# Merging the routing scores with the expert activation stage: one block, shared buffers, and GpSimd's subtract cut in four

## The reference, cut to what matters

```python
q = (xb @ wq).reshape(PEER_BLOCK, PEER_HEADS, 2, PEER_HALF)
s = jnp.einsum('thpd,hpkd->thpk', q, subkeys).astype(jnp.float32)
s_top, i_top = lax.top_k(s, PEER_TOPK)
cand = (s_top[:, :, 0, :, None] + s_top[:, :, 1, None, :]).reshape(...)
g_s, g_i = lax.top_k(cand, PEER_TOPK)
e = jnp.take_along_axis(cand_idx, g_i, axis=-1)
g = jax.nn.softmax(g_s, axis=-1).astype(xb.dtype)
act = jax.nn.gelu(jnp.einsum('thed,td->the', u[e], xb))
return jnp.einsum('the,thed->td', g * act, v[e])
```

## Time and profile before

| | |
|---|---|
| median of 3 runs | 2461.23 us (2456.18 to 2461.99) |
| the profiled execution | 2459.62 us, its span 2458.0 us |
| mean granted clock of TensorE | 0.909 |
| busy: PE, PEld, DVE, ACT, POOL | 86%, 69%, 68%, 35%, 38% of the span |
| scores, activation, experts | about 940 to 1108, 1108 to 1897, 1897 to 2458 us |

### The profile page before, as it was taken

How to read it: one execution, slowest core, us unless ns; L and a number is a source line. 1 busy time by engine, 2 the same in 40 slices (tenths; PEclk the granted TensorE clock), 3 DMA queues, 4 the chain that set the end, 5 groups by cost and what they waited for, 6 DMA issues and landing times. The chain is left out here.

```text
span 2458.0 us, 32103 instructions
## 1 busy us (share of the span) xinstructions
PE 2118.9 (86%) x10417; PEld 1703.5 (69%) x10417; DVE 1667.0 (68%) x2980; ACT 853.3 (35%) x1717; POOL 942.2 (38%) x727
## 2 busy tenths in 40 slices
PE   8998986687987767979799889887886999999997
PEld 7774773343435636859798889877885788888885
DVE  3562106868230133797989999988665898898888
ACT  1231012133100121113566576546553333333331
POOL 1000342222100000014677677766676566444440
PEclk9999997678899678989899999998997999999998
DMA  5323438866604102126687788778888999999993
GB/s 189 77 55 110 130 97 285 295 211 216 244 23 143 56 0 75 61 69 193 193 278 263 251 260 278 264 235 268 279 286 281 394 388 391 395 389 389 385 386 131
DMA packets 243759, 547.72 MB, mean 223 GB/s; under 512 B 22174, under 2 KB 126287, under 8 KB 242346
## 3 DMA queue, kind: packets, MB, share of 16 engines
q1 hardware_dynamic: 114538, 287.33, 33.9%
q0 software_dynamic: 60736, 208.40, 23.5%
q10 hardware_dynamic: 68352, 50.34, 6.3%
HBM read 485.51 MB, written 60.02 MB: 222 GB/s over the span
## 5 line engine op out<-in xcount | busy, mean ns | idle before, releaser
L2404 PE MATMUL psum<-hH,uH 128*128 128x384 f32 x1024 | 365.3, 357 | 76.7 <-ACT acts L2218 36.2
L2079 POOL DMA_INDIRECT u_gather<-in_u_rows,gather_ids x160 | 218.4, 1365 | 546.6 <-DVE gather_ids L1889 419.3
L2196 POOL TENSOR_TENSOR uL<-u_raw,uH 128x1024 fp32r<-128x1024 f32 x125 | 320.6, 2565 | 129.5 <-ACT uH L2210 126.3
L2404 PE MATMUL psum<-hL,uH 128*128 128x384 f32 x1024 | 355.4, 347 | 0.0
L2404 PE MATMUL psum<-hH,uL 128*128 128x384 f32 x1024 | 355.2, 347 | 0.0
L2301 DVE CUSTOM_DVE_ANT_0 u_prod<-u_gather,h 128x1024 f32<-128x1024 f32 x160 | 283.6, 1773 | 81.8 <-DMA u_gather<-in_u_rows,gather_ids 73.6
L2512 POOL DMA_INDIRECT v_gather<-in_v_rows,idx_now x160 | 237.9, 1487 | 247.1 <-DVE y_sample L2597 154.7
L2644 PE MATMUL psum<-vH,wH 128*128 128x512 f32 x768 | 301.9, 393 | 18.0 <-DVE wL L2590 18.0
L2644 PE MATMUL psum<-vH,wL 128*128 128x512 f32 x768 | 301.2, 392 | 0.0
L2644 PE MATMUL psum<-vL,wH 128*128 128x512 f32 x768 | 301.0, 392 | 0.0
L2404 PEld LDWEIGHTS psum<-hH,uH 128*128 128x128 f32 x1024 | 203.4, 199 | 82.9 <-issue 60.4
(11 more groups left out here) (485 smaller groups left out, 3463.2 us busy)
## 6 DMA issues: line engine op xcount, KB each, us to landing
u_raw<-in_uT SPq DMA_DIRECT2D x128, 512.0 KB, 4.4
S<-in_v_rows SPq DMA_DIRECT2D x64, 512.0 KB, 10.6
v_rest<-in_v_rows SPq DMA_DIRECT2D x64, 512.0 KB, 6.7
activation_table<-acts ACTq DMA_DIRECT2D x128, 192.0 KB, 4.2
gate_table<-Gtile ACTq DMA_DIRECT2D x48, 512.0 KB, 8.0
S<-gate_table SPq DMA_DIRECT2D x16, 768.0 KB, 8.0
S<-activation_table SPq DMA_DIRECT2D x16, 768.0 KB, 11.8
G_rest<-gate_table SPq DMA_DIRECT2D x16, 768.0 KB, 7.4
```

Of the source, the lines that this page charges most:

```text
L2079: c.nc.gpsimd.indirect_dma_start(c.ug[:, k % RG], None, c.A["u_rows"].rearrange("j i d -> (j i) d"), bass.IndirectOffsetOnAxis(ap=c.ids[:, ...
L2196: nc.gpsimd.tensor_tensor(uL[:, n % RU], u[:, n % RAW], uH[:, n % RU].bitcast(F32), ALU.subtract).then_inc(u_split, 1)
L2404: ins = nc.tensor.matmul(bank[n % 2][:, 0:ND], w[:, n % RU, d], x[:, d], start=m == 0, stop=m == len(parts) - 1)
```

## The change: what it does

- `stage_scores` becomes `score_programs`, which returns one function for each engine. `stage_activate` calls them at the start of its own block, so that no engine waits for the others between the scores and the activation. `hT` stays until the end of the activation.
- To make room, tensors share buffers: `wq`, `subkeys`, `qp` and `S_first` lie in `Gtile`; `hot` and `S_first_last` in `hT`; `slot_ij`, `slot_gate`, `res` and `idf` in constants that are no longer used. The product of a dot is written over the fetched row instead of to `u_prod`. Two waits are added for it: ScalarE waits for `h_split` ahead of the last head's first score copy, VectorE for the last `s_ev` ahead of the activation.
- `RG` is 5, so five fetches can be under way.
- `column`: the columns' sums use four PSUM banks (0, 1, 6, 7) in turn and not two; TensorE waits for the gelu of four columns before.
- `low_u`: GpSimd's subtract of a column, 128 x 1024, becomes four of 128 x 256. The semaphore counts behind the last.
- `STEP_COLS`: tile 0 has 12 columns and not 8, tile 3 has 28 and not 32.
- `tile_gates(0)` moves from step 5 of tile 0 to step 7.

```diff
-STEP_COLS = ((1,) * 8, (5, 5, 5, 5, 5, 5, 4, 4), (5,) * 8, (4,) * 8)
+STEP_COLS = ((2, 1) * 4, (5, 5, 5, 5, 5, 5, 4, 4), (5,) * 8, (4, 3) * 4)
...
-RG = 4
+RG = 5
...
+def low_u(c, n):
+
+    for d in range(0, KD, 2):
+        ins = c.nc.gpsimd.tensor_tensor(c.uL[:, n % RU, d:d + 2], c.u[:, n % RAW, d:d + 2],
+                                        c.uH[:, n % RU, d:d + 2].bitcast(F32), ALU.subtract)
+    ins.then_inc(c.u_split, 1)
...
-        slot_ij, slot_g, prod = sb("slot_ij", [P, PUNIT, 2, UNIT]), sb("slot_gate", [P, 2, P]), sb("u_prod", [P, D])
+        slot_ij = c.bcol[:].rearrange("p b n -> p (b n)").rearrange("p (u q t) -> p u q t", u=PUNIT, q=2)
+        slot_g = [c.tri, c.low]
...
+        pool_scores, sp_scores, pe_scores, act_scores, dve_scores = score_programs(
+            c, G[:].rearrange("p a j t -> p (a j t)"))
+        column = [bank[i] for i in (0, 1, 6, 7)]
...
-                    routed = st == (0 if p else 5)
+                    routed, gates = st == (0 if p else 5), st == (0 if p else 7)
...
-                        if routed and i == 1:
+                        if gates and i == 1:
                             tile_gates(p)
...
             @block.gpsimd
             def _(pool):
+                pool_scores(pool)
+
                 def columns(n):
                     n += AHEAD
                     if n < NKEYS:
                         pool.wait_ge(u_hi, n + 1)
-                        nc.gpsimd.tensor_tensor(uL[:, n % RU], u[:, n % RAW], uH[:, n % RU].bitcast(F32),
-                                                ALU.subtract).then_inc(u_split, 1)
+                        low_u(c, n)
...
-                    V.tensor_tensor_reduce(out=prod[:], in0=c.ug[:, k % RG], in1=c.h[:, STILE if s == GS else 0],
+                    V.tensor_tensor_reduce(out=c.ug[:, k % RG], in0=c.ug[:, k % RG], in1=c.h[:, STILE if s == GS else 0],
...
                 def columns(n):
                     pe.wait_ge(u_split, n + 1)
-                    if n >= 2:
-                        pe.wait_ge(u_act, n - 1)
+                    if n >= 4:
+                        pe.wait_ge(u_act, n - 3)
...
-            stage_scores(c)
-            hTs.close()
             stage_activate(c)
+        hTs.close()
         stage_experts(c)
```

More of the change, by code:

```diff
@@ new lines, in score_programs @@
+    sizes = (RING * KD * P, NJ * NKEYS, 2 * NT, 2 * ROUTED * NKEYS)
+    ends = list(itertools.accumulate(sizes))
+    part = [room[:, end - n:end] for n, end in zip(sizes, ends)]
+    wq = part[0].rearrange("p (i k n) -> p i k n", i=RING, k=KD)
+    sk = part[1].rearrange("p (j n) -> p j n", j=NJ)
+    qp = part[2].rearrange("p (i n) -> p i n", i=2)
+    S0 = part[3]
+    SS = c.route.SS
+    sk_in, q_mm, q_ev = c.sem("sk_in"), c.sem("rq_mm"), c.sem("rq_ev")
+    wq_in = [c.sem(f"wq_in{i}") for i in range(RING)]
@@ new lines, in pe_scores, with scores @@
+    def pe_scores(pe):
+        def scores(j):
+            pe.wait_ge(q_ev, j + 1)
+            if j == 0:
+                pe.wait_ge(sk_in, 16)
+            if j >= 2:
+                pe.wait_ge(s_ev, 2 * (j - 1))
+            quarter = slice(j // 2 % 4 * NS, (j // 2 % 4 + 1) * NS)
+            for t in range(NTILE):
+                dst = bank[4 + j % 2][:, t * P:(t + 1) * P] if t < STILE else bank[6 + j % 2][quarter, 0:P]
+                ins = nc.tensor.matmul(dst, qp[:, j % 2, cols(t)], sk[:, j], start=True, stop=True)
+            ins.then_inc(s_mm, 1)
+        for j in range(NJ):
+            pe.wait_ge(wq_in[j % RING], 16 * (j // RING + 1))
+            if j >= 2:
+                pe.wait_ge(q_ev, j - 1)
+            for q in range(2):
+                for k in range(KD):
+                    ins = nc.tensor.matmul(c.pair(j % 2)[:, q], wq[:, j % RING, k],
+                                           c.hT[:, k, q * HALF:(q + 1) * HALF],
+                                           start=k == 0, stop=k == KD - 1)
+            ins.then_inc(q_mm, 1)
+            if j:
+                scores(j - 1)
+        scores(NJ - 1)
@@ new lines, in dve_scores @@
+    def dve_scores(dve):
+        V = nc.vector
+        for k in range(KD):
+            V.tensor_copy(hH[:, k], c.hT[:, k, P:SEQ]).then_inc(h_split, 1)
+            dve.wait_ge(h_split, 2 * k + 1)
+            V.tensor_tensor(hL[:, k], c.hT[:, k, P:SEQ], hH[:, k].bitcast(F32), ALU.subtract).then_inc(h_split, 1)
+        dve.wait_ge(h_split, 2 * KD)
+        b = c.route
+        router = Router(c, dve, Link(dve, d_own))
+        for h in range(ROUTED):
+            dve.wait_ge(s_ev, 4 * (h + 1))
+            keys = slice(h * 2 * NKEYS, (h + 1) * 2 * NKEYS)
+            router.head(S0[:, keys], b.first, h, c.res0)
+            router.head(S[:, 0, keys], b.second, h, b.res)
+            if h == BATCH - 1:
+                router.convert(b.first, BATCH)
+                for i in range(BATCH):
+                    router.pick(i, c.res0)
+                router.rows_of(c.res0, 0, 64, c.ids[:, 0:NG // 2, 0:GS])
+                router.convert(b.second, BATCH)
+                for i in range(BATCH):
+                    router.pick(i, b.res)
+                router.head(SS[:, 0], b.sample, 0, c.resS)
+        dve.wait_ge(s_ev, 4 * PH)
@@ L2037 @@
+    return pool_scores, sp_scores, pe_scores, act_scores, dve_scores
 TB = 32
@@ L2217, in columns @@
                         act.wait_ge(a_stored[n % RA], 16 * (n // RA))
-                    nc.scalar.activation(a[:, n % RA], bank[n % 2][:, 0:ND], ACT.Gelu_apprx_tanh).then_inc(u_act, 1)
+                    nc.scalar.activation(a[:, n % RA], column[n % 4][:, 0:ND], ACT.Gelu_apprx_tanh).then_inc(u_act, 1)
                     act.wait_ge(u_act, n + 1)
```

186 lines of the change are left out of this document (64 added, 122 removed).

## The result

| | us |
|---|---|
| before, median of 5 runs | 2461.23 (2456.18 to 2462.75) |
| after, median of 5 runs | 2436.57 (2435.52 to 2445.76) |
| ratio, with its 95% interval | 0.992 [0.9894, 0.9941]: faster, by 0.6 to 1.1% |
| forecast | 2407 (2350 to 2447) |
| after, profiled span, mean granted clock | 2434.7, 0.919 |

A forecast was written before the change was run, and what follows sets the result against it. The prediction took VectorE, sharing an exclusive SBUF port with GpSimd, as the bound, TensorE second. From 2459.6 us it took 14.5 for the start and 38 for tiles 1 to 3, giving 2407 us, range 2350 to 2447.

The forecast's parts named there:

- The seam: Between scores and activation: TensorE runs nothing for 16 us; merging the blocks lets columns start at about 1092 us.
- D: Rival on the subtract's pieces: they do nothing, each port wait still lasts a whole subtract; 2429 us, chance 0.16.
- Start-up: Up to tile 1's transposes: merged blocks start columns earlier, transposes end at 1182.4 instead of 1196.9 us; gain 14.5 us.
- Tiles 1 to 3: Rest of the activation stage, 701 us: pieces let VectorE and GpSimd fill each other's port gaps; 663 us, gain 38.
- 15 us for the pieces' own cost: Tiles 1 to 3: the pieces' fixed cost, 0 to 61 us, mostly hidden while VectorE has the port; a quarter taken.
- 10 us of fetch waits: Tiles 1 to 3: VectorE's waits for fetched rows fall from 74 us as a fifth buffer lets fetches run ahead.
- the 2452 us: Time forecast if the pieces' fixed cost, 187 ns by a rule from the Trainium skill, were exposed in full, 60 us.
- The fifth buffer: Fetched rows, mainly tile 3: lets GpSimd run one dot further ahead; counted as 10 us in D.
- Four banks: Column sums in PSUM: remove 36 us of TensorE's waits for ScalarE's column activation, but priced at 0.
- TensorE isn't last: Tiles 1 to 3: TensorE's own 531 us lie under the 663 us forecast, so its waits don't set the time.
- Rival C: GpSimd becomes the bound, its pieces queueing behind VectorE's instructions: 727 us for tiles 1 to 3, 2471 in all, chance 0.15.
- B: Rival: the hand-over works better, common off-port time falls to 30 us and the pieces' cost vanishes; 2349 us, chance 0.14.

The follow-up runs named there:

- iota in PSUM: The changed kernel, four pieces, with VectorE's one-hot builds reading iota from a PSUM bank into which ScalarE copies it once: 2410.7 us.
- fetch ahead, one: The changed kernel with GpSimd's fetch issued ahead of its column's subtract, and the subtract in one piece: 2410.1 us.
- fetch ahead, two: The changed kernel with GpSimd's fetch issued ahead of its column's subtract, and the subtract in two pieces: 2400.2 us.
- fetch ahead, four: The changed kernel, four pieces, with only GpSimd's order turned round, the fetch ahead of the subtract: 2427.2 us.
- fetch ahead and iota, two: The changed kernel with the subtract in two pieces, the fetch ahead of it, and one-hot builds reading iota from PSUM: 2366.4 us.
- fetch ahead and iota, four: The changed kernel, four pieces, with the fetch ahead of the subtract and one-hot builds reading iota from PSUM: 2395.0 us.

## Why the prediction was partly right

**Right.** The bound: VectorE and GpSimd on one port, TensorE second. The seam: columns at 1092.4 (forecast about 1092), worth 16 us by itself. The wait ahead of the gates is gone. The time fell, as forecast, and the experts are within 3 us. D's mechanism is out as a whole: pieces hand the port over most of the time; but 14 instructions met it. Its outcome for the pieces, that they gain nothing, was near.

**Start-up, forecast 14.5 us, measured 8.8.** From the first column matmul to the transposes the forecast had 21 x 4.16 + 1.5 = 88.9 us; it took 95.1. The changed kernel's trace shows what the 6 us are, GpSimd and TensorE in order of time and then the busy times of 6 us:

```profile
1168.89 1.42 POOL L2079 DMA_INDIRECT u_gather<-in_u_rows,gather_ids  x1 [6.14 <-DVE dots L2320]
1170.33 5.87 POOL L2087 TENSOR_TENSOR uL<-u_raw,uH 128x256 fp32r<-128x256 f32 x4
...
1176.25 0.69 PE L2425 MATMUL psum<-hH,uH 128*128 128x384 f32 x1 [2.92 <-POOL uL L2087]
...
1176.00:1182.00 6.00, 5.75 (x18) 5.75 (x19) 4.97 (x19) 1.06 (x1) 5.66 (x7) 0.50 0.54 180
```

GpSimd's fetch waited 6.14 us for a dot, and the four pieces behind it took 5.87 us, as VectorE's dots got the port in between. So TensorE waited 2.92 us for uL, and behind this pause its granted clock was 0.50 for about 6 us, the 1.2 GHz level: its matmuls started every 0.32 us and not every 0.17. With two pieces the fetch waited 6.13 us too, but the two pieces took 2.53 us, TensorE was busy in all of the stretch, and it took 90.0 us. The waits that the pieces moved to GpSimd reached TensorE here. This is one profile of each kernel; others with 21 columns had 90 to 99 us.

**Tiles 1 to 3, forecast 38 us, measured 11.5: the steps that failed are "15 us for the pieces' own cost" and "10 us of fetch waits".** The forecast took the pieces to be worth 22 us (its 2407 against D's 2429). The runs give 1 us (2436.6 against 2437.7). It priced their cost at a quarter of the upper end, since "most of it hides while VectorE has the port". Two pieces run back to back in 2.49 us and four in 2.80, one in 2.34: 0.15 us for each further one. The trace shows the 2.49 in this row of the two-piece kernel, GpSimd in order of time:

```profile
1186.30 2.49 POOL L2087 TENSOR_TENSOR uL<-u_raw,uH 128x512 fp32r<-128x512 f32 x2
```

In 107 columns four pieces take GpSimd 107 x 0.46 = 49 us more than one. How much of that shows can be read from the traces: *in use* below is the time in tiles 1 to 3 in which a subtract of GpSimd or a dot or other two-operand elementwise instruction of VectorE is in progress (working or waiting for the other; one-hots with iota in PSUM left out), *neither* is the remainder. "Subtracts" is 107 times (110 in the kernel before) the shortest duration of a column's subtract, and the last column VectorE's waits for rows.

| kernel | tiles 1 to 3 | subtracts | in use | neither | waits for rows |
|---|---|---|---|---|---|
| before | 700.8 | 257 | 546.0 | 154.8 | 73.6 |
| one piece | 686.7 | 250 | 537.5 | 149.2 | 68.0 |
| two | 680.6 | 266 | 546.0 | 134.6 | 83.1 |
| four (the change) | 689.3 | 300 | 563.4 | 125.8 | 139.8 |
| fetch ahead, one | 654.1 | 250 | 536.5 | 117.6 | 33.9 |
| fetch ahead, two | 649.5 | 266 | 545.1 | 104.4 | 46.1 |
| fetch ahead, four | 682.9 | 300 | 565.8 | 117.1 | 118.4 |
| fetch ahead and iota, two | 616.3 | 266 | 467.1 | 149.2 | 49.6 |
| fetch ahead and iota, four | 648.4 | 300 | 497.8 | 150.6 | 137.3 |

Of the 49 us, 26 show as time in which the port's users are at work (537.5 to 563.4), where the sum had 15; about half hides, where the forecast had most of it. Against it the time of neither fell by 23 us (149.2 to 125.8), and the two cancel. The forecast had 251 + 300 + 15 = 566 us for the first, which the measured 563.4 meets partly by luck: with one piece it was 13.5 us less than 251 + 300 already. For the second it had 73 + 13.6 + 10 = 97 us, and that is where the distance lies: 125.8. VectorE working off the port makes 37 of it (forecast 73; 80 before), and waiting for rows 64 (forecast 10; 49 before); the rest is shorter waits, 7 us for the last exponential among them.

From two to four pieces the timed kernels lose 27 us with the fetch ahead and 29 with iota in PSUM too. In their profiles the first loss is 21 us of use and 13 us of neither, the second 31 us of use. So from one piece to two the relief is larger than the price, and from two to four it is smaller. The table has one profile for each kernel.

With the full price, 46 to 49 us where the sum had 15, the forecast would be 2438 to 2441, near the measured 2436.6; by the table that agreement is luck. The same holds for the 2452 us that the prediction gave beside it. That estimate was worked out from the 4497 ns for 2048 elements of the Trainium skill (GPSIMD Engine Reference, "3.1 Elementwise"); the 187 ns of fixed cost that follow are near the 0.15 us of these runs, but in the changed kernel they aren't exposed in full.

**"10 us of fetch waits", measured 139.8 in all.** Its picture was that a fetch is late for want of a buffer. What stands ahead of the fetch makes it late, a column's subtract that now keeps GpSimd 3.95 us and not 2.57: 68.0 us of waits with one piece, 83.1 with two and 139.8 with four. And there is a circle; in tile 3 of the changed kernel, in order of time:

```profile
1702.19 0.69 ACT L2279 ACTIVATE hT<-hT,tri 128x128 f32<-128x128 f32 x2 [8.14 <-DVE hT L2348]
...
1703.56 1.04 ACT L2227 ACTIVATE uH<-u_raw 128x1024 fp32r<-128x1024 f32 x1
...
1704.67 3.44 POOL L2087 TENSOR_TENSOR uL<-u_raw,uH 128x256 fp32r<-128x256 f32 x4 [5.52 <-ACT uH L2227]
...
1708.25 0.94 POOL L2079 DMA_INDIRECT u_gather<-in_u_rows,gather_ids  x1
...
1713.90 1.64 DVE L2320 CUSTOM_DVE_ANT_0 u_gather<-u_gather,h 128x1024 f32<-128x1024 f32 x1 [8.45 <-DMA u_gather<-in_u_rows,gather_ids]
...
1715.47 1.48 DVE L2348 TENSOR_TENSOR hT<-iota,bcol 128x768 f32<-128x768 f32 x1
...
1716.98 0.69 ACT L2279 ACTIVATE hT<-hT,tri 128x128 f32<-128x128 f32 x2 [6.09 <-DVE hT L2348]
```

ScalarE's gate multiply waits 8.14 us for a one-hot; the next uH stands behind it; GpSimd's subtract waits 5.52 us for that uH; the fetch stands behind the subtract; VectorE waits 8.45 us for the row; the next one-hot stands behind that dot; and ScalarE waits again, 6.09 us. Each engine works in order, and the circle closes. Tile 3 holds 103.2 of the 139.8 us and didn't get shorter with four columns less. The circle existed before the change (20 us from the order alone); the forecast took most of its waits as recoverable by the buffer, and the pieces lengthened them. Issuing the fetch ahead cuts the circle, but with four pieces 118 us of waits stay, so there GpSimd's load is most of the cause.

**Terms too low.** The fifth buffer: 10 us forecast (in D), 14 measured. Four banks: 0 forecast, 7 measured, not clear of the noise; undone, TensorE waits 27.5 us for ScalarE's column activation again, though 25.7 instead of 53.1 for uL. "TensorE isn't last" was too coarse: at tile 1's start it is, where VectorE waits 6.81 us for its transposes.

**Rival C** was nearer in its signs than in its time. GpSimd came to 0.90 of tiles 1 and 2, VectorE waited for rows and TensorE for uL. But GpSimd's subtracts lost 134 us to VectorE where C had 174, and of the pieces' cost 26 us showed where C had 61. **B**'s off-port time of 30 us was never reached; the lowest was 104.

**The best version** has the merge and the side parts of the change, two pieces, the fetch ahead of the subtract, and iota in PSUM: 2366.4 us, 70 us faster than the change and 94 faster than before.

## What to carry to other kernels

Cutting an instruction on a shared port buys shorter waits with a fixed cost for each piece, and it shortens one engine's waits by lengthening the other's: multiply that cost by the number of pieces, expect half of it or more to show when both engines are nearly full, look for what waits behind the engine that got slower, and try two pieces before four. Here taking one operand off the port was worth more (26 us) than slicing (1 to 10 us). Where an engine waits for data that another queue fetches, look at what stands ahead of the fetch in that queue and what that in turn waits for; if it leads back to the first engine, put the fetch ahead.

## What the runs showed of the hardware

- Back-to-back pieces of GpSimd hand the port over in most cases, not in all: at 1317.15 a VectorE comparison waited through four pieces, and at 1157.07 one took 6.24 us for 0.7, longer than the eight pieces beside it (5.6 us). 12 of the 14 long waits began within 0.08 us of the start of a piece. Whether that decides it wasn't tried.
- A subtract of 128 x 1024 takes GpSimd 2.34 us, two of 512 take 2.49 and four of 256 take 2.80: 0.15 us for each further instruction.
- Not only instructions with two operands in SBUF wait: a cast of 128 x 128 by VectorE (L1873 of the kernel before, 0.23 us at least) took 3.05 us at 1275.99, to 0.1 us behind the end of GpSimd's subtract.
- With one of two operands in PSUM, 96 one-hot builds of VectorE had a mean of 949 ns beside GpSimd's subtracts, equal to their shortest; with both in SBUF 1282 to 1677. Here the Trainium skill (SBUF — State Buffer, "Who interferes with whom") agrees: it counts an instruction of VectorE as contending when two of its inputs are in SBUF.
